# Feeding the high and low activations behind one load of the high weights, in the down products of 256 tokens

## The reference

```
def _swiglu(x, w_up, w_down):
    a, b = jnp.split(x @ w_up, 2, axis=-1)
    return (jax.nn.silu(a) * b) @ w_down
```

## Time and profile before

| | us |
|---|---|
| median of 3 runs | 1674.0 |
| lowest, highest | 1671.62, 1680.55 |
| the profiled execution's own time | 1677.43 |
| its span, first to last instruction | 1675.7 |

### The profile page before, as it was taken

The page is one execution under the profiler, slowest core; times in us unless marked ns, Lnnn a source line. Parts: engine busy times, 40 slices in busy tenths (PEclk is TensorE's granted clock), DMA queues, the critical chain, the costliest instruction groups (busy, mean ns, idle before and its releaser), DMA issues. The chain is left out here.

```text
span 1675.7 us, 33814 instructions
## 1 busy us (share of the span) xinstructions
PE 1554.0 (93%) x14238; PEld 1498.5 (89%) x14238; DVE 1045.2 (62%) x1583; ACT 740.7 (44%) x1017; POOL 61.5 (4%) x82
## 2 busy tenths in 40 slices
PE   3999998989999898999989899999999898899997
PEld 2999998989999798999979899899999787799997
DVE  6999547986664758444488653555444677655544
ACT  2545434783212744444446020466433445456532
POOL 0121000000000000110000000000000000000000
PEclk7999999998989999999999998999999999999999
DMA  9799645432211445554533000344444332135551
GB/s 361 289 338 337 240 170 187 173 143 104 75 64 56 165 170 204 199 190 172 177 135 119 9 2 1 101 160 171 156 172 146 123 113 101 51 133 194 177 200 50
DMA packets 39195, 256.78 MB, mean 153 GB/s; under 512 B 4259, under 2 KB 5668, under 8 KB 9892
## 3 DMA queue, kind: packets, MB, share of 16 engines
q1 hardware_dynamic: 37492, 251.07, 41.9%
q10 hardware_dynamic: 1584, 3.97, 0.6%
HBM read 251.87 MB, written 3.15 MB: 152 GB/s over the span
## 5 line engine op out<-in xcount | busy, mean ns | idle before, releaser
L471 DVE TENSOR_TENSOR w_lo<-raw,w_hi 128x2048 fp32r<-128x2048 f32 (+2 forms) x203 | 456.5, 2249 | 411.2 <-ACT w_hi L463 410.9
L555 PE MATMUL bank<-x_hi,w_hi 128*128 128x256 f32 (+1 forms) x1832 | 526.6, 287 | 30.5 <-DVE x_lo L730 12.2
L463 ACT ACTIVATE w_hi<-raw 128x2048 fp32r<-128x2048 f32 (+2 forms) x203 | 381.9, 1881 | 336.2 <-PE bank L557 298.3
L557 PE MATMUL bank<-x_hi,w_lo 128*128 128x256 f32 (+1 forms) x1832 | 518.3, 283 | 0.0
L556 PE MATMUL bank<-x_lo,w_hi 128*128 128x256 f32 (+1 forms) x1832 | 517.7, 283 | 0.0
L555 PEld LDWEIGHTS bank<-x_hi,w_hi 128*128 128x128 f32 x1832 | 347.5, 190 | 37.6 <-issue 24.1
L557 PEld LDWEIGHTS bank<-x_hi,w_lo 128*128 128x128 f32 x1832 | 349.2, 191 | 0.0
L556 PEld LDWEIGHTS bank<-x_lo,w_hi 128*128 128x128 f32 x1832 | 347.8, 190 | 0.9 <-issue 0.7
L555 PE MATMUL bank<-mh_hi,w_hi 128*128 128x272 f32 (+1 forms) x512 | 145.2, 284 | 5.3 <-issue 5.3
L556 PE MATMUL bank<-mh_lo,w_hi 128*128 128x272 f32 (+1 forms) x512 | 145.7, 285 | 0.0
L557 PE MATMUL bank<-mh_hi,w_lo 128*128 128x272 f32 (+1 forms) x512 | 145.2, 284 | 0.0
(11 more groups left out here) (578 smaller groups left out, 2534.0 us busy)
## 6 DMA issues: line engine op xcount, KB each, us to landing
raw<-in_stream SPq DMA_DIRECT2D x227, 1024.0 KB, 4.8
raw<-in_stream SPq DMA_DIRECT2D x8, 768.0 KB, 4.2
gate_store<-stage ACTq DMA_DIRECT2D x8, 256.0 KB, 2.2
raw<-in_stream SPq DMA_DIRECT2D x4, 512.0 KB, 3.5
h<-in_h ACTq DMA_DIRECT2D x1, 1088.0 KB, 6.5
zt<-gate_store SPq DMA_DIRECT2D x1, 1024.0 KB, 5.7
gate<-gate_store SPq DMA_DIRECT2D x1, 1024.0 KB, 7.9
out<-h SPq DMA_DIRECT2D x8, 128.0 KB, 1.9
```

The costliest lines, as they stand in the source:

```text
L463: nc.scalar.activation(w_hi[:, s_at % 2, 0:kt], raw[:, r_at % RING, 0:kt], ACT.Copy).then_inc(hi_done, 1)
L471: nc.vector.tensor_tensor(w_lo[:, s_at % 2, 0:kt], raw[:, r_at % RING, 0:kt], w_hi[:, s_at % 2, 0:kt].bitcast(F32), ALU.subtract).then_inc ...
L555: nc.tensor.matmul(out, hi, xh[:, k0 + k, 0:L], start=start, stop=False)
L557: mm = nc.tensor.matmul(out, lo, xh[:, k0 + k, 0:L], start=False, stop=stop)
```

## The change

In `down1`, `down2` and `mlp2_1` (256 tokens), the high and low activations become one tensor with two halves, and one matmul of 512 columns moves both behind one load of `w_hi`. Its result fills the whole bank: the part from the high activations in columns 0 to 255, that from the low ones in columns 256 to 511. The matmul of `w_lo` adds to columns 0 to 255 as before. VectorE now has two halves of each output to bring together. `residual` does its two instructions on the first halves, waits for them, and does two more on the second halves. `scaled` multiplies both halves of both outputs (four instructions), waits, and adds the two products with one instruction of 512 elements. `mlp2_0` keeps its three products.

```
-        def pe_pairs(pe, sec, xh, xl, L, after=None, norm=None, tile_ready=None, U=2, busy=0, begun=()):
+        def pe_pairs(pe, sec, xh, xl, L, after=None, norm=None, tile_ready=None, U=2, busy=0, begun=(), both=None):
...
-                        nc.tensor.matmul(out, hi, xh[:, k0 + k, 0:L], start=start, stop=False)
-                        nc.tensor.matmul(out, hi, xl[:, k0 + k, 0:L], start=False, stop=False)
+                        if both is not None:
+                            two = out_bank(sec, u, j)[:, 0:2 * L].rearrange("p (a n) -> p a n", a=2)
+                            nc.tensor.matmul(two, hi, both[:, :, k0 + k], start=start, stop=False)
+                        else:
+                            nc.tensor.matmul(out, hi, xh[:, k0 + k, 0:L], start=start, stop=False)
+                            nc.tensor.matmul(out, hi, xl[:, k0 + k, 0:L], start=False, stop=False)
                         mm = nc.tensor.matmul(out, lo, xh[:, k0 + k, 0:L], start=False, stop=stop)
...
-                hid_hi = sb(f"hid_hi{q}", [P, FF1T, L], F32R, c)
-                hid_lo = sb(f"hid_lo{q}", [P, FF1T, L], F32R, c)
+                hid_both = sb(f"hid_both{q}", [P, 2, FF1T, L], F32R, c)
+                hid_hi, hid_lo = hid_both[:, 0], hid_both[:, 1]
...
+                            ins.then_inc(halved, 1)
+                            dve.wait_ge(halved, u + 1)
+                            for j in range(2):
+                                k = 2 * u + j
+                                ins = nc.vector.scalar_tensor_tensor(
+                                    out=h1[:, k], in0=out_bank(down, u, j)[:, L:2 * L], scalar=gain_col[:, k:k + 1], in1=h1[:, k],
+                                    op0=ALU.mult, op1=ALU.add)
                             ins.then_inc(dve_took, 1)
...
-                                 tile_ready=lambda k: pe.wait_ge(hid_l, k + 3))
+                                 tile_ready=lambda k: pe.wait_ge(hid_l, k + 3), both=hid_both[:])
...
-                hid_hi = sb(f"mh_hi{layer}", [P, FF2T, L], F32R, c)
-                hid_lo = sb(f"mh_lo{layer}", [P, FF2T, L], F32R, c)
+                hid_both = sb(f"mh_both{layer}", [P, 2, FF2T, L], F32R, c)
+                hid_hi, hid_lo = hid_both[:, 0], hid_both[:, 1]
+                wide = L == T1
+                total = sb(f"total{layer}", [P, 2, L], c=c) if wide else None
...
                             for j in range(2):
-                                ins = nc.vector.tensor_tensor(out[:, 2 * u + j], out_bank(down, u, j)[:, 0:L], rr[:], ALU.mult)
+                                if wide:
+                                    ins = nc.vector.tensor_tensor(out[:, 2 * u + j], out_bank(down, u, j)[:, 0:L], rr[:], ALU.mult)
+                                    nc.vector.tensor_tensor(total[:, j], out_bank(down, u, j)[:, L:2 * L], rr[:], ALU.mult).then_inc(halved, 1)
+                                else:
+                                    ins = nc.vector.tensor_tensor(out[:, 2 * u + j], out_bank(down, u, j)[:, 0:L], rr[:], ALU.mult)
+                            if wide:
+                                dve.wait_ge(halved, 2 * u + 2)
+                                ins = nc.vector.tensor_tensor(out[:, 2 * u:2 * u + 2], out[:, 2 * u:2 * u + 2], total[:], ALU.add)
                             ins.then_inc(dve_took, 1)
...
-                        pe_pairs(pe, down, hid_hi, hid_lo, L, tile_ready=lambda k: pe.wait_ge(s_lo, 2 + k // 2 + 1))
+                        pe_pairs(pe, down, hid_hi, hid_lo, L, tile_ready=lambda k: pe.wait_ge(s_lo, 2 + k // 2 + 1), both=hid_both[:] if wide else None)
```

More of the change, by code:

```diff
@@ L1140, in swiglu @@
             L = T1
-            gated, hid_h, hid_l = (sem(f"{x}{q}") for x in ("gated", "hid_h", "hid_l"))
+            gated, hid_h, hid_l, halved = (sem(f"{x}{q}") for x in ("gated", "hid_h", "hid_l", "halved"))
             with ExitStack() as c:
-                hid_hi = sb(f"hid_hi{q}", [P, FF1T, L], F32R, c)
-                hid_lo = sb(f"hid_lo{q}", [P, FF1T, L], F32R, c)
+                hid_both = sb(f"hid_both{q}", [P, 2, FF1T, L], F32R, c)
+                hid_hi, hid_lo = hid_both[:, 0], hid_both[:, 1]
                 act_out = sb(f"act_out{q}", [P, 2, L], c=c)
@@ L2927, in mlp @@
                 mid = over_x[:, 1, :, 0:L]
-                s_sq, s_hi, s_lo = (sem(f"{x}{layer}") for x in ("mlp_sq", "mlp_hi", "mlp_lo"))
+                s_sq, s_hi, s_lo, halved = (sem(f"{x}{layer}") for x in ("mlp_sq", "mlp_hi", "mlp_lo", "mlp_halved"))
                 with nc.Block() as block:
```

## The result

| | before | after |
|---|---|---|
| median, us | 1674.24 (8 runs, 1671.24 to 1702.69) | 1689.53 (8 runs, 1682.03 to 1716.28) |
| profiled execution, us | 1677.43 | 1688.66 |
| its span, us | 1675.7 | 1686.9 |

The ratio is 1.0088, with a 95% interval from 1.0060 to 1.0116: slower by the prediction's line of 0.5%, where 1675.2 and "no change" were forecast.

The account below looks back on a forecast made before the run. Matmul pace on TensorE was taken to bound the three stages. Costs of 5.4 us less 396 S, with S = 0.0107 us, gave +1.2 us: profiled 1677.4 to 1678.6, forecast median 1675.2, range 1668.5 to 1682.

Parts of the forecast that it names:

- the chain take, square, `w_hi`, `w_lo`: In `mlp2_1`, takes 1.41 us longer delay `w_lo`; TensorE waits 0.65, 0.65 and 1.25 us before third slabs, 2.55 together.
- the room in `down1`: Third slab due at 209.5, its `w_lo` ready at 207.8, so a take 0.91 us longer fits without a wait.
- Their sum, 5.4: Cost in us without S: +0.91 in `down1`, +0.5 in `down2`, +2.55 and +1.41 in `mlp2_1`.
- I read the 113.3 as set by the load, and take 216 ns for the wide product: Three stages: wide product 216 ns plus `w_lo` product 113.3 make 329.3, against a triple of 340 before.
- S: Time saved in each triple of products in `down1`, `down2` and `mlp2_1`, forecast as 10.7 ns.
- the prediction's formula: Whole change over the three stages: 5.4 - 396 S, with S in us; at S = 0.0107, +1.2 us.
- Rival 1: No saving per column in the three stages, S = 0: +5.4 us, 1679.4; chance 0.17.
- Rival 2: Moving operand in two distant pieces is slow, S = -17: +12.1 us, 1686.1; chance 0.09.
- Rival 3: Both products at bare columns, S = 20: -2.5 us, 1671.5; chance 0.08 together with rival 4.
- rival 4: Stalls in `mlp2_1` don't come, the chain takes up 1.41 us: 1671.6; chance 0.08 together with Rival 3.
- Rival 5: Pace drawn anew at waits, also in later sections: 4.4 us either way on 1000 matmuls; chance 0.16, half each way.
- if sections without a change move by more than 2 us: Sign for the prediction being wrong, beside the wide product taking over 234 ns.

Follow-up runs that it names:

- `split_out`: Kernel before, still three 256-column products, but the low one goes to columns 256 to 511 and VectorE does the changed kernel's longer takes: 1679.66 us, ratio 1.0042.
- experiment 4: Kernel before with rows of filler products of several widths into an unused bank behind `mlp2_1`, twice over: 512 columns every 233.3 ns, 384 every 174.7.
- experiment 1: Changed kernel with high and low activations interleaved by k-tile, so the 512 columns lie in one piece: twelve pairs again 4.24 us; 1706.17 us, ratio 1.0196.
- `wide_first`: Changed kernel with wide products and longer takes in `down1` and `down2` alone, `mlp2_1` as before: 1697.58 us, ratio 1.0081.
- `wide_last`: Changed kernel with wide products and longer takes in `mlp2_1` alone, `down1` and `down2` as before: 1678.16 us, ratio 1.0013.
- `ruler`: The kernel of experiment 4: kernel before plus filler rows of several widths behind `mlp2_1`; 512 columns every 233.3 ns, 128 every 111.7.
- `ruler_2`: Kernel before plus rows of 16 filler products behind `mlp2_1`, varying start address, load size, weights or type: 512 columns 233.5 ns, 228.5 from 64 bytes later.

## Why the prediction was wrong

**What held.** That matmul pace bounds the three stages; 13630 matmuls; the take of `mlp2_1` (2.14 us, forecast 2.16), that of `down1` (+0.91 exactly); the chain take, square, `w_hi`, `w_lo` in `mlp2_1` that has no slack, with waits of 0.54 and 1.14 (forecast 0.65 and 1.25) in `split_out`; the room in `down1`. Their sum, 5.4, wasn't measured by itself: that the median of `split_out` moved by 4.7 is luck, as its profile shows 10 us more in the touched stretches and 9 less in the others.

**The step that failed** is "I read the 113.3 as set by the load, and take 216 ns for the wide product". The wide product measured 235 ns in the kernel and the `w_lo` product behind it 118, so S = -13 instead of +10.7: 0.024 x 396 = 9.4 us of the error. The prices came from fp32 rows of 512 columns, where a record takes 429.2 ns against 426.7 of bare columns and is only half a matmul, while the fast type has a surplus on every column (0.458 ns instead of 0.417): rows of another type priced the one number that mattered. The reading of 113.3 as the price of the load is in doubt too. The 111.7 ns of 128 columns show that short products with a load each don't come faster than some 112 ns, as the 1-column rows said. But wide products, with half as many loads a column, settled at 226 to 227 ns in experiment 4, which is 2 x 113.3. That speaks for 113.3 as a pace of 256 columns that lies near the 112 by chance; no row changes the load of a 256-column product, so this isn't shown. Why the fast type's columns have two paces, and why the wide form holds the slower one in the kernels, stays open.

With S = -13 the prediction's formula gives 5.4 + 396 x 0.013 = 10.5 us. The touched stretches grew by 10.3 in the profiled executions, the whole by 11.2. In `mlp2_1` the slower triples cover part of the waits: 32 triples before the slab take 0.42 us longer, and 0.65 - 0.42 = 0.23 and 1.25 - 0.42 = 0.83 stand against 0.10 and 0.70 in the trace, some 0.12 less, as in `split_out`. By the formula the median would have been 1684.5, 5 us under the measured one. Most of that is where the profiled executions lie among the runs: that of before 3.2 us above its median, that of after 0.9 below. Without the three runs at the lower clock the median of after would be 1688.7, so they are not what made the forecast wrong.

**The rivals.** Rival 1 had the mechanism, surplus per column, but put S at 0, since it left both forms at one pace. Where the three products themselves run at 117.7 S is indeed 0; most of these stages ran at 113.3. Rival 2 had nearly the size (S = -17) and its bound of 234 ns was passed, but pieces weren't the cause (experiment 1). Rival 3 is out, and rival 4 too: the waits came in `split_out`. Rival 5 is real and as large as said (3.4 us in one stage of `wide_first`). The chance of "slower", 0.10, was too low because rivals 1 and 5 were priced apart: S = 0 with both forms at the same pace, S = -13 with the old form at the faster pace and the wide one at the slower, which is how most of the touched stages ran in the two profiles.

**What stood in no part of it** is the long stretch at half clock. The prediction's own sign for being wrong, "if sections without a change move by more than 2 us", did not show between the two profiled executions (1.1 us at most), but it did in `split_out` (6.0 and 6.2 us less, from shorter stretches at half clock) and in every profile with the long stretch (18 to 25 us more between `down2` and `mlp2_0`). The runs of the changed kernel with the lower clock lie 12 us above its others.

No kernel with a part of the change is faster than the one before: `wide_last` comes nearest, with an interval from 0.9978 to 1.0047.

## What to carry to other kernels

Price a wider matmul by its columns in its own type: get ns per column from two widths of that type, or measure a row of it, before counting a load saved as time saved. Here it paid nothing, because the wide stream was bound by its columns, at 0.456 ns each. Merging products moves work to whoever takes the result out, and where that take stands ahead of the next slab's split in a chain without slack, what it adds reappears in the bound engine as a wait. A median that moves by the forecast amount is no proof of the terms: look whether the stages of the change moved, as `split_out` shows. And a stage that isn't touched can change by many microseconds, so look at the mean granted clock of every run, not only at the profiled one.

## What the runs showed of the hardware

- With a load ahead of each product, at full granted clock, the fast type moves 512 columns in 233 to 235 ns, 384 in 174.7, 256 in 117.8 and 128 in 111.7 (`ruler`, `ruler_2`).
- There is a second, faster pace: 113.3 ns for 256 columns and 226 to 227 for 512. The same row of products settled at it in one lap of `ruler` and not in the other. The old stream held either pace for a whole stage of 87 or 90 us (before, `wide_first`), and changed it at short waits of TensorE.
- A plain fp32 matmul of 512 columns is two records with a load each, 429.2 ns a record, 858 ns in all (`ruler_2`).
- A load of 32 columns instead of 128 ahead of a 512-column product changes it by 2 ns (231.2 against 233.5).
- In a stage of small matmuls with TensorE almost always busy the granted clock fell to 0.5 for 41 to 65 us in four of the profiled executions and for at most 14 us at a time in the others.
